# The residual addition of tiles four to eight moves from VectorE to GpSimd

## The chip, the cores and the metric

The kernel runs on one core of one Trainium2 chip. A core has five engines with queues of their own: TensorE (PE in the profile, with its weight loads as PEld), VectorE (DVE), ScalarE (ACT), GpSimd (POOL) and SyncE (SP, which only issues transfers here). They run side by side and wait for each other through semaphores. The metric is the device time of one execution in microseconds (us), the median of several runs.

## The reference, cut to what matters

One inference step of a two-layer backbone, on 256 context tokens and 1024 latent tokens of width 1024, in float32. Each layer ends its mixer with an output projection, a gated residual, a norm and an expert-choice router:

```python
out = jnp.concatenate([y_h, y_a], axis=-1) @ e_w_out[a]      # layer 0; layer 1: o @ r_w_out[r]
x = x + g_a * out                                            # gate product, residual addition
hn = rms_norm(x, norm_ffn_g[l]) * (1.0 + sc_f) + sh_f
x = x + g_f * expert_choice_ffn(hn, router_w[l], moe_w_gu[l], moe_w_down[l])

def expert_choice_ffn(h, router_w, w_gu, w_down):
    cap = CAPACITY_FACTOR * n // N_EXPERTS                   # 2 * n / 16 tokens per expert
    aff = jax.nn.softmax((xf @ router_w).astype(jnp.float32), axis=-1)
    gate, idx = lax.top_k(aff.T, cap)                        # each expert picks its tokens
    xin = xf[idx]
    ...
```

Context and latent tokens are routed apart, so the kernel has three lists to sort: latent tokens in two halves, and context tokens.

## The kernel before, in words

`out_proj_route` is called twice, once per layer, and each call is one stage. It works on ten tiles of 128 tokens: tiles 0 to 3 are the first half of the latent tokens, 4 to 7 the second, 8 and 9 the context. For tile n the engines do this, in turn:

- TensorE projects the tile into a PSUM buffer (line 1415, two buffers in turn).
- VectorE multiplies it with the gate into `xn` (line 1473, semaphore `products`) and adds the residual into `x` (line 1476, semaphore `gated`); the two are `gate_add(n)`. `xn` has two buffers and `x` three.
- ScalarE issues the store of `x` (line 1597), squares and sums it (line 1600), and takes the root (line 1606).
- VectorE inverts the root (line 1480, `invert(n)`).
- ScalarE scales `x` into `xn` again (line 1608, semaphore `scaled`). `xn` then holds the normalised tile.
- GpSimd stores `xn` to HBM (line 1347), and TensorE transposes it (line 1363), for the router's matmuls (line 1376).

After four tiles the router's logits go through a softmax: VectorE lines 1489 to 1497, where `aff_ready` is given, TensorE `to_experts` (line 1392), and VectorE's copy into the work area (line 1504). Then VectorE picks each expert's best tokens, eight at a time: a round is MAX8, FIND_INDEX8 and MATCH_REPLACE8 (lines 1513 to 1515). There are 16 rounds for the first half and 16 for the second, in which the context's list is sorted along.

No scheduler sets the order. Each engine's list is written out by hand, and an engine does its list in order. VectorE's list from tile five on stands in these lines of the kernel before:

```python
            rounds(0, 0, 3)
            gate_add(5)
            rounds(0, 3, 4)
            invert(5)
            rounds(0, 4, 9)
            gate_add(6)
            rounds(0, 9, 10)
            invert(6)
            rounds(0, 10, 15)
            gate_add(7)
            invert(7)
```

Then come the last round of the first half, the second softmax, `gate_add(8)`, the copy `to_work(1)`, `invert(8)`, and the second half's rounds with `gate_add(9)` and `invert(9)` between them. GpSimd has nothing in the stage but the ten stores and, at the end, two gathers by the picked indices (lines 1352 and 1354), with which the expert stage begins.

Of the kernel before, what the change touches and what calls it, by code (L numbers as in the profile page):

```python
# [16 lines left out]
ALU = mybir.AluOpType  # L17
# [1234 lines left out]
PICKS = [(0, CAP[1], CT * P), (CAP[1], CAP[1], (CT + 4) * P), (2 * CAP[1] - CAP[0], CAP[0], 0)]  # L1252
CTX = slice(2 * NE, 3 * NE)
ROUTE_AT = 158016


def out_proj_route(nc, A, S, tag, w, w_in, early_gate, lhs, lhs_in, x_in, x_out, layer, hnT, xn_dram, router, idx, idx_four, gates,
# [4 lines left out]
    NB = 3  # L1262
    NPICK = 2 * CAP[1]
    with ExitStack() as ctx:
        _, ps, sem = scope(nc, ctx, tag)

        def fixed(name, shape, offset, dt=F32):
            return nc.alloc_sbuf_tensor_at(f"{tag}_{name}", shape, dt, offset=offset)
# [3 lines left out]
        x = fixed("x", [P, NB, D], 100672)  # L1272
        xn = fixed("xn", [P, 2, D], 112960)
        junk = fixed("junk", [P, D], 121152)
        work = fixed("work", [3 * NE, LL], ROUTE_AT)
        top = fixed("top", [3 * NE, NPICK], ROUTE_AT + 5120)
        topi = fixed("topi", [3 * NE, NPICK], ROUTE_AT + 6272, U32)
        topf = fixed("topf", [3 * NE, NPICK], ROUTE_AT + 7424)
        back_a = fixed("back_a", [NE, 2, CAP[1]], ROUTE_AT + 8576)
        ge, val, ind = (fixed(n, [NE, CAP[1]], ROUTE_AT + 9600 + 512 * i) for i, n in enumerate(("ge", "val", "ind")))  # L1280
        aff = fixed("aff", [P, 4, NE], ROUTE_AT + 11136)
# [10 lines left out]
        eps_ready, mm, products, gated, squared, v_steps, inverted, rooted, scaled, tr, hn_out = (sem(n) for n in (  # L1292
            "eps_ready mm products gated squared v inverted rooted scaled tr hn_out").split())
        lg_zero, lg_mm, lt_out, tk_tr, subbed, exped, aff_ready, back, worked, a_ready, a_turned, context_turned, picked, finals, idx_ready = (sem(n) for n in (
            "lg_zero lg_mm lt_out tk_tr subbed exped aff_ready back worked a_ready a_turned context_turned picked finals idx_ready").split())
        x_ins, stored = [sem(f"x_in{i}") for i in range(NB)], [sem(f"stored{i}") for i in range(NB)]
# [12 lines left out]
        def tokens(n):  # L1309
            return slice(TILES[n] * P, (TILES[n] + 1) * P)  # L1310
# [4 lines left out]
        @block.sync  # L1315
        def _(sp):
            load_router_w(sp, A, router, layer)
            for n in range(NT):
                if n >= NB:
                    sp.wait_ge(stored[n % NB], 16 * (n // NB))  # L1320
                    sp.wait_ge(scaled, n - NB + 1)
                sp.dma_start(x[:, n % NB, :], x_in(TILES[n])).then_inc(x_ins[n % NB], 16)
                if n == NB:
                    for j in range(4):
                        load_expert(sp, A, layer, expert_w, expert_w_in, j, 0)
            def load_mod(n):
                if n >= 4:
                    sp.wait_ge(mod_used, n - 3)
                src = (A["mod_w"][shift_of, n * P:(n + 1) * P, 0:2048] if n < KD else
                       A["mod_b"][shift_of:shift_of + 1, 0:2048].broadcast_to([P, 2048]))  # L1330
                sp.dma_start(ring[n % 4][:, :, :].rearrange("p j n -> p (j n)"), src).then_inc(mod_in[n % 4], 16)

            if shift_of:
                load_mod(0)
                load_mod(1)
            sp.wait_ge(mm, NT)
            if shift_of:
                for n in range(2, KD + 1):
                    load_mod(n)
            for j in range(4, 9):  # L1340
                load_expert(sp, A, layer, expert_w, expert_w_in, j, 0)

        @block.gpsimd
        def _(pool):
            for n in range(NT):
                pool.wait_ge(scaled, n + 1)
                pool.dma_start(xn_dram[tokens(n), :], xn[:, n % 2, :]).then_inc(xn_stored[n % 2], 16)
            for i in range(2):
                pool.wait_ge(xn_stored[i], 16 * len(range(i, NT, 2)))
            xl, xc, xl_in, xc_in = first  # L1350
            pool.wait_ge(idx_ready, 1)
            pool.indirect_dma_start(xc[:, :], None, xn_dram, bass.IndirectOffsetOnAxis(idx_four[:, 0:1], 0)).then_inc(xc_in, 16)
            pool.wait_ge(idx_ready, 2)
            pool.indirect_dma_start(xl[:, :], None, xn_dram, bass.IndirectOffsetOnAxis(idx[1][:, 0:1], 0)).then_inc(xl_in, 16)
# [110 lines left out]
        def _(dve):  # L1465
            steps = Count(v_steps)

            def gate_add(n):
                dve.wait_ge(mm, n + 1)
                if n >= 2:  # L1470
                    dve.wait_ge(tr, n - 1)
                    dve.wait_ge(xn_stored[n % 2], 16 * (n // 2))
                nc.vector.tensor_tensor(xn[:, n % 2, :], psm[n % 2][:, :], gate[:, 0 if TILES[n] < CT else 1, :], ALU.mult).then_inc(products, 1)
                dve.wait_ge(products, n + 1)
                dve.wait_ge(x_ins[n % NB], 16 * (n // NB + 1))
                nc.vector.tensor_tensor(x[:, n % NB, :], xn[:, n % 2, :], x[:, n % NB, :], ALU.add).then_inc(gated, 1)
# [66 lines left out]
            for n in range(5):  # L1543
                gate_add(n)
                invert(n)
            subtract_max(0)
            shares(0)
            to_work(0)
# [8 lines that stand above are left out]
# [28 lines left out]
            for c in (1, 0):  # L1585
                n = CAP[c]
# [1201 lines left out]
```

## Time and profile before

| | us |
|---|---|
| median of 3 runs (lowest, highest) | 4161.03 (4160.32, 4161.28) |
| the profiled execution's own time | 4160.97 |
| its span in the profile | 4159.2 |
| PE busy | 3887.9 (93%) |
| DVE busy | 1741.3 (42%) |
| ACT busy | 1139.9 (27%) |
| POOL busy | 201.2 (5%) |

The first stage's tiles run from about 905 to 1058 us of the span, the second's from about 3098 to 3240 us. The shares are means over the whole span. In the stages they are others, and what counts there is which wait ends last.

### The profile page before, as it was taken

How to read it: one execution, taken by the hardware profiler on the slowest of the kernel's cores; microseconds unless marked ns; L12 is line 12 of the kernel's file. 1: busy time of each engine (PE TensorE's matmuls, PEld its weight loads, DVE VectorE, ACT ScalarE, POOL GpSimd, SP SyncE). 2: the span in 40 equal slices, each digit the busy share in tenths (PEclk: the TensorE clock that was granted, in tenths of full speed). 3: DMA queues.
4: the chain of work that ended last, by engine and by line, in shares of the span. 5: the costliest groups of instructions: out<-in, count | busy, mean ns of one | idle time of the engine just before them, and what ended most of it. 6: DMA issues, size and time to landing. Idle time of an engine off the chain costs nothing. (4 is left out here: it accounts for less than half of the span.)

```text
span 4159.2 us, 56347 instructions
## 1 busy us (share of the span) xinstructions
PE 3887.9 (93%) x24035; PEld 3135.7 (75%) x24035; DVE 1741.3 (42%) x2860; ACT 1139.9 (27%) x2162; POOL 201.2 (5%) x237
## 2 busy tenths in 40 slices
PE   7999989999799999999899999999879599999998
PEld 3444456654599999997788888888854599999997
DVE  3325457745411111111368788888875411111112
ACT  4010135533201111110444555445534211011112
POOL 1010000000000000000000000000000000000000
PEclk9999989999899999999899999999999899999999
DMA  5432010023888888887210100100223688888886
GB/s 191 142 124 75 16 51 1 1 87 112 278 255 258 260 254 259 253 255 243 80 29 29 30 29 17 35 29 25 83 87 112 207 260 256 262 252 260 252 257 238
DMA packets 507896, 617.88 MB, mean 149 GB/s; under 512 B 17282, under 2 KB 467508, under 8 KB 501632
## 3 DMA queue, kind: packets, MB, share of 16 engines
q1 hardware_dynamic: 482400, 518.89, 38.5%
q0 software_dynamic: 21984, 84.77, 7.3%
q10 hardware_dynamic: 3264, 10.63, 0.6%
q8 instruction: 191, 3.13, 0.3%
q14 instruction: 57, 0.47, 0.0%
HBM read 561.08 MB, written 53.15 MB: 148 GB/s over the span
## 5 line engine op out<-in xcount | busy, mean ns | idle before, releaser
L1855 PEld LDWEIGHTS moe_pgu<-step_hnT,expert_w 128*128 128x128 f32 x8192 | 1113.6, 190 | 20.5 <-issue 20.5
L1855 PE MATMUL moe_pgu<-step_hnT,expert_w 128*128 128x160 f32 x8192 | 1121.7, 299 | 7.3 <-DVE moe_hT L2001 4.2
L2001 DVE TENSOR_TENSOR moe_hT<-moe_sg,moe_pgu 128x160 f32<-128x160 f32 x256 | 82.1, 321 | 968.7 <-PE moe_pgu L1855 959.2
L1867 PE MATMUL moe_pol<-expert_w,moe_hT 128*128 128x256 f32 x2048 | 457.5, 381 | 2.4 <-DVE moe_hT L2001 1.0
L1922 ACT ACTIVATE moe_sg<-moe_pgu 128x160 f32<-128x160 f32 x256 | 77.5, 303 | 1303.4 <-PE moe_pgu L1855 1291.4
L2205 PE MATMUL l_psm<-step_hnT,rec_w 128*128 128x256 f32 x1920 | 425.7, 380 | 3.5 <-ACT l_zc L2288 1.9
L1867 PEld LDWEIGHTS moe_pol<-expert_w,moe_hT 128*128 128x128 f32 x2048 | 383.2, 190 | 59.1 <-DVE moe_hT L2001 10.0
L2205 PEld LDWEIGHTS l_psm<-step_hnT,rec_w 128*128 128x128 f32 x1920 | 362.1, 191 | 51.6 <-ACT l_zc L2288 2.3
L2209 PE MATMUL l_psm<-rec_w,step_hnT 128*128 128x256 f32 x1280 | 282.4, 379 | 0.0
L2209 PEld LDWEIGHTS l_psm<-rec_w,step_hnT 128*128 128x128 f32 x1280 | 240.4, 190 | 31.3
L2013 DVE SCALAR_TENSOR_TENSOR moe_ol<-moe_pol,step_gates,moe_gate_f 128x512 f32<-128x512 f32 x64 | 48.1, 751 | 434.6 <-PE moe_pol L1867 434.6
L2246 PE MATMUL rec_pg<-rec_ring 128*128 128x128 f32 x1600 | 195.4, 280 | 27.8 <-DVE rec_tot L2422 22.2
L2246 PEld LDWEIGHTS rec_pg<-rec_ring 128*128 128x128 f32 x1600 | 189.5, 195 | 40.9 <-issue 32.7
L530 PE MATMUL hin_psm<-step_hnT,hin_w 128*128 128x512 f32 (+1 forms) x576 | 215.9, 531 | 2.7 <-DVE step_hnT L634 2.7
L530 PEld LDWEIGHTS hin_psm<-step_hnT,hin_w 128*128 128x128 f32 x576 | 109.3, 193 | 110.2 <-issue 87.4
L1905 ACT ACTIVATE step_hnT<-moe_pxt,step_modcol 128x128 f32<-128x128 f32 x288 | 108.2, 456 | 177.2 <-PE moe_pxt L1828 177.2
L2543 DVE COPY_PREDICATED rec_AT<-rec_maskb,rec_pg 128x512 f32<-128x512 uint8 (+1 forms) x192 | 109.9, 627 | 46.9 <-PE rec_pg L2246 45.4
L1786 POOL DMA_INDIRECT scratch_xm<-moe_ol,step_idx x31 | 49.1, 1585 | 1443.2 <-DVE moe_ol L2013 1443.2
L1877 PE MATMUL moe_poc<-expert_w,moe_hT 128*32 128x256 f32 x2048 | 117.1, 380 | 0.0
L1118 PE MATMUL att_to_ps<-step_ident,l0a_p 128*128 128x128 f32 x672 | 100.1, 287 | 12.1 <-issue 11.0
L1179 DVE TENSOR_REDUCE att_nmax<-att_s_ps 128x1 f32<-128x1280 f32 (+1 forms) x80 | 99.1, 1274 | 26.6 <-PE att_s_ps L1100 26.1
L1118 PEld LDWEIGHTS att_to_ps<-step_ident,l0a_p 128*128 128x128 f32 x672 | 73.0, 144 | 42.0 <-issue 29.6
(444 smaller groups left out, 4439.5 us busy)
## 6 DMA issues: line engine op xcount, KB each, us to landing
expert_w<-in_moe_w_gu SPq DMA_DIRECT2D x256, 1024.0 KB, 10.4
expert_w<-in_moe_w_down SPq DMA_DIRECT2D x128, 1024.0 KB, 13.4
late_w<-in_mod_w POOLq DMA_DIRECT2D x24, 1024.0 KB, 5.2
rec_w<-in_r_w_in SPq DMA_DIRECT2D x40, 512.0 KB, 3.9
scratch_xm<-op_x ACTq DMA_DIRECT2D x20, 512.0 KB, 2.6
scratch_xn<-op_xn POOLq DMA_DIRECT2D x20, 512.0 KB, 5.5
mod_w<-in_mod_w SPq DMA_DIRECT2D x8, 1024.0 KB, 16.4
op_mod<-in_mod_w SPq DMA_DIRECT2D x8, 1024.0 KB, 7.9
```

What stands on the lines that cost most here:

```text
L530: m = nc.tensor.matmul(psm[j % NPS][:, 0:n * P], w[:, i % 2, k, part, :], hnT[:, k, t0 * P:(t0 + n) * P], start=(k == 0), stop=(k == KD - 1))
L1118: m = nc.tensor.transpose(bank("t", i, g)[:, n * P:(n + 1) * P], p[:, i % 2, r, a * P:(a + 1) * P], S["ident"][:, :])
L1179: nc.vector.tensor_reduce(nmax[:, x:x + 1], s_ps[:, r, 0:nk * P], AX_X, ALU.max, negate=True).then_inc(maxed, 1)
L1855: m = nc.tensor.matmul(pgu[2 * (f % 2) + part][:, :], w[j][:, k, (f % 2) * P:(f % 2 + 1) * P], ring[:, k, e % 8, :], start=(k == 0), stop= ...
L1867: m = nc.tensor.matmul(pol[q // 2][:, (q % 2) * SW:(q % 2 + 1) * SW], hT[:, k, 0:CL], w[8 + q][:, k, :], start=(k == 0), stop=(k == KD - 1))
L1877: m = nc.tensor.matmul(poc[32 * q:32 * q + CP, :], hT[:, k, CL:CC], w[8 + q][:, k, :], start=(k == 0), stop=(k == KD - 1), tile_position=( ...
L1905: r = nc.scalar.activation(dst, src, ACT.Identity, bias=mc[:, layer, 3, c, k:k + 1], scale=mc[:, layer, 4, c, k:k + 1])
L2001: nc.vector.tensor_tensor(hT[:, f, :], sg[:, f % 2, :], pgu[2 * (f % 2) + 1][:, :], ALU.mult).then_inc(multiplied, 1)
L2205: m = nc.tensor.matmul(pz[i % 3][:, 0:2 * P], w[:, k, n // NZU, :], hnT[:, k, c0:c0 + 2 * P], start=(k == 0), stop=(k == KD - 1))
L2209: m = nc.tensor.matmul(pz[i % 3][:, 0:2 * RD], hnT[:, k, t * P:(t + 1) * P], w[:, k, 3:5, :].rearrange("p a c -> p (a c)"), start=(k == 0) ...
L2246: into_banks(h, (d, i), lambda o, t: nc.tensor.matmul(o, kb[:, t * P:(t + 1) * P], qb[:, t * P:(t + 1) * P], start=True, stop=True))
L2543: last = nc.vector.copy_predicated(at, maskb[:, j:j + 1, :].broadcast_to([P, nt, P]), src)
```

## The change

`POOL_ADDS` names tiles 4 to 8. For those, GpSimd does the residual addition in front of its store of the same tile, waiting for the gate product and for the loaded residual. VectorE's `gate_add` returns after the gate product. Everything else in VectorE's list keeps its place. Before the addition of tile 9, VectorE waits for `gated` of tile 8, which keeps the count of that semaphore in order.

```diff
+POOL_ADDS = range(4, 9)
...
             for n in range(NT):
+                if n in POOL_ADDS:
+                    pool.wait_ge(products, n + 1)
+                    pool.wait_ge(x_ins[n % NB], 16 * (n // NB + 1))
+                    nc.gpsimd.tensor_tensor(x[:, n % NB, :], xn[:, n % 2, :], x[:, n % NB, :], ALU.add).then_inc(gated, 1)
                 pool.wait_ge(scaled, n + 1)
                 pool.dma_start(xn_dram[tokens(n), :], xn[:, n % 2, :]).then_inc(xn_stored[n % 2], 16)
...
                 nc.vector.tensor_tensor(xn[:, n % 2, :], psm[n % 2][:, :], gate[:, 0 if TILES[n] < CT else 1, :], ALU.mult).then_inc(products, 1)
+                if n in POOL_ADDS:
+                    return
+                if n - 1 in POOL_ADDS:
+                    dve.wait_ge(gated, n)
                 dve.wait_ge(products, n + 1)
                 dve.wait_ge(x_ins[n % NB], 16 * (n // NB + 1))
                 nc.vector.tensor_tensor(x[:, n % NB, :], xn[:, n % 2, :], x[:, n % NB, :], ALU.add).then_inc(gated, 1)
```

VectorE's list in the first stage, before, from the third round to the fifth, around tile five (`op_xn<-op_psm,op_gate` is the gate product, `op_x<-op_xn,op_x` the addition, `op_rstd` the inverted root):

```order
L1515 MATCH_REPLACE op_work<-op_top,op_work 16x512
L1473 TENSOR_TENSOR op_xn<-op_psm,op_gate 128x1024
L1476 TENSOR_TENSOR op_x<-op_xn,op_x 128x1024
L1513 MAX op_top<-op_work 16x8
L1514 MAX_INDEX op_topi<-op_top,op_work 16x8
L1515 MATCH_REPLACE op_work<-op_top,op_work 16x512
L1480 RECIPROCAL op_rstd<-op_ssq 128x1
```

The same place now (the lines count nine or five more):

```order
L1524 MATCH_REPLACE op_work<-op_top,op_work 16x512
L1478 TENSOR_TENSOR op_xn<-op_psm,op_gate 128x1024
L1522 MAX op_top<-op_work 16x8
L1523 MAX_INDEX op_topi<-op_top,op_work 16x8
L1524 MATCH_REPLACE op_work<-op_top,op_work 16x512
L1489 RECIPROCAL op_rstd<-op_ssq 128x1
```

The addition is gone from between the product and the fourth round, and the reciprocal still stands behind that round. It is the same at tile six, and at tiles seven and eight no round stands between.

GpSimd's list in the first stage now, from its start to the second addition (`scratch_xn<-op_xn` is the store; before, the ten stores stood in one piece):

```order
L1352 DMA scratch_xn<-op_xn 128x1024 x4
L1350 ISA
L1350 TENSOR_TENSOR op_x<-op_xn,op_x 128x1024
L1352 DMA scratch_xn<-op_xn 128x1024
L1350 TENSOR_TENSOR op_x<-op_xn,op_x 128x1024
L1352 DMA scratch_xn<-op_xn 128x1024
```

Each addition stands right in front of the store of its own tile. The row ISA in front of the first addition is new, and the second stage has none.

## Rows read from the trace of the kernel before

**Rows 1.** Waits of DVE, 980 to 1045 us: total, times, longest
```profile
DVE op_stat L1489 <- PE op_tok L1382: 8.9, 1, 8.9
DVE op_rstd L1480 <- ACT op_ssq L1606: 5.8, 3, 2.7
```

**Rows 2.** Timeline of DVE, first stage: start, us, what [idle before <-releaser]
```profile
963.67 1.23 DVE L1473 TENSOR_TENSOR op_xn<-op_psm,op_gate 128x1024 f32<-128x1024 f32 x1 [10.04 <-PE op_psm L1415]
...
971.49 0.23 DVE L1497 TENSOR_TENSOR op_aff<-op_aff,op_stat 128x64 f32<-128x64 f32 x1
...
983.76 1.22 DVE L1473 TENSOR_TENSOR op_xn<-op_psm,op_gate 128x1024 f32<-128x1024 f32 x1
985.02 1.22 DVE L1476 TENSOR_TENSOR op_x<-op_xn,op_x 128x1024 f32<-128x1024 f32 x1
...
989.51 0.16 DVE L1480 RECIPROCAL op_rstd<-op_ssq 128x1 f32<-128x1 f32 x1 [1.23 <-ACT op_ssq L1606]
...
1004.88 0.16 DVE L1480 RECIPROCAL op_rstd<-op_ssq 128x1 f32<-128x1 f32 x1
...
1020.11 0.16 DVE L1480 RECIPROCAL op_rstd<-op_ssq 128x1 f32<-128x1 f32 x1 [1.91 <-ACT op_ssq L1606]
...
1035.78 0.67 DVE L1504 COPY op_work<-op_pback 16x512 f32<-16x512 f32 x1
1039.13 0.16 DVE L1480 RECIPROCAL op_rstd<-op_ssq 128x1 f32<-128x1 f32 x1 [2.68 <-ACT op_ssq L1606]
```

**Rows 3.** Timeline of ACT, first stage
```profile
986.28 0.33 ACTq L1597 DMA_DIRECT2D scratch_xm<-op_x  x1
...
989.71 1.15 ACT L1608 ACTIVATE op_xn<-op_x,op_rstd 128x1024 f32<-128x1024 f32 x1 [0.30 <-DVE op_rstd L1480]
...
1004.40 0.30 ACT L1606 ACTIVATE op_ssq<-op_ssq,op_eps 128x1 f32<-128x1 f32 x1
...
1019.78 0.29 ACT L1606 ACTIVATE op_ssq<-op_ssq,op_eps 128x1 f32<-128x1 f32 x1
```

**Rows 4.** Timeline of PE, first stage and the expert stage's first transposes
```profile
975.95 0.60 PE L1392 MATMUL op_pback<-step_ident,op_aff 128*16 128x128 f32 x4
...
1007.21 3.60 PE L1415 MATMUL op_psm<-op_w,l_filt 128*128 128x512 f32 x8
...
1021.50 1.27 PE L1363 MATMUL op_pst<-step_ident,op_xn 128*128 128x128 f32 x8 [3.83 <-ACT op_xn L1608]
1022.57 5.16 PE L1415 MATMUL op_psm<-op_w,l_filt 128*128 128x512 f32 x8
...
1094.10 1.09 PE L1837 MATMUL moe_pxt<-step_ident,first_xc 128*128 128x128 f32 x4 [10.73 <-PEq L80]
```

**Rows 5.** Timeline of POOL, first stage
```profile
955.11 0.53 POOL L1347 DMA_DIRECT2D scratch_xn<-op_xn  x1 [14.08 <-ACT op_xn L1608]
...
991.15 0.53 POOL L1347 DMA_DIRECT2D scratch_xn<-op_xn  x1 [20.90 <-ACT op_xn L1608]
...
1084.44 1.03 POOL L1352 DMA_INDIRECT first_xc<-scratch_xn,step_idx_four  x1 [25.09 <-DVE step_idx L1587]
```

**Rows 6.** Windows: us, PE, PEld, DVE, ACT, POOL busy (x), PEclk, DMA, GB/s
```profile
1021.50:1026.00 4.50, 4.50 (x13) 2.57 (x14) 1.22 (x5) 2.90 (x8) 0.53 (x1) 0.62 0.29 117
1026.00:1031.00 5.00, 5.00 (x73) 2.83 (x72) 0.00 (x0) 1.32 (x2) 0.00 (x0) 1.00 0.01 3
```

**Rows 7.** Timeline of DVE, second stage: reciprocals of tiles five, six and eight
```profile
3171.63 0.16 DVE L1480 RECIPROCAL op_rstd<-op_ssq 128x1 f32<-128x1 f32 x1 [1.23 <-ACT op_ssq L1606]
...
3187.00 0.16 DVE L1480 RECIPROCAL op_rstd<-op_ssq 128x1 f32<-128x1 f32 x1
...
3221.10 0.16 DVE L1480 RECIPROCAL op_rstd<-op_ssq 128x1 f32<-128x1 f32 x1 [2.67 <-ACT op_ssq L1606]
```

**Rows 8.** Tile op_x, and groups of DVE by form: durations in ns
```profile
L1476 DVE TENSOR_TENSOR op_x<-op_xn,op_x x20: 1224/1225/1226, 906.6 to 3235.3; 128x1024 f32<-128x1024 f32 x20
...
L2458 DVE TENSOR_TENSOR_SCAN rec_X<-rec_restart,l_zc 128x1280 f32<-128x1280 uint8 x16 | 45.2, 2825 | 0.6
```

## The prediction

> **What bounds the kernel now.** I read the timelines of the five engines over the first stage first, then the waits of VectorE, then the same places in the second stage, and last the prices of single instructions. I name tiles from zero, as the code does.
>
> The reader is to see one chain of waits through the tiles five to eight, and to ask at each reciprocal whether VectorE came late or early. The chain is: gate product, residual addition, store issue, square and root on ScalarE, reciprocal on VectorE. VectorE's list is in order, so the rounds behind a reciprocal start only when it is done. At tile five the addition starts at 985.02, ScalarE issues the store at 986.28, and VectorE, done with its fourth round, idles 1.23 us before the reciprocal at 989.51 until the root is there [rows 2, 3]. At tile seven it idles 1.91 us and at tile eight 2.68 us for the same reason [rows 2]. These three make the 5.8 us that VectorE waits for roots in this stretch [rows 1]. At tile six it idles nothing: the root ends at 1004.70 and the reciprocal starts at 1004.88, while at tile seven it starts 0.04 us behind its root (1020.07 to 1020.11) [rows 2, 3]. So the root had only some 0.14 us to spare at tile six. VectorE is busy there, and yet the additions are not what holds it: the chain to the root is.
>
> What is late next is read from PE. It idles 3.83 us until `xn` of tile seven is scaled, and only then transposes it [rows 4]. Behind that stand the router's matmuls of the second half, and VectorE idles 8.9 us for them [rows 1]. So a delay at tiles five, six and seven goes on through PE to the second softmax and to tile eight's product. A delay at tile eight goes on through the reciprocal to the second half's rounds, to the indices, to GpSimd's first gather (1084.44) [rows 5], and to the expert stage, whose first transposes start at 1094.10 [rows 4]. From there on PE is the busy engine, so I count every microsecond at the stage's end as one at the program's end. The second stage shows the same idle times: 1.23 us at tile five, none at six, 2.67 us at eight [rows 7].
>
> **The change part by part.** Removed from VectorE: five additions a stage, each 1.225 us [rows 8]. I cost this at nothing gained. The rounds that move up end earlier and then wait for the root, as the rows say they do already at tile five; at tile six the freed time becomes a wait as well, beyond the 0.14 us; at tiles seven and eight nothing but the copy into the work area stands between product and reciprocal.
>
> Added to the chain: the way over GpSimd. Before, from the end of the product (983.76 plus 1.22, so 984.98) to ScalarE's store issue (986.28) it is 1.30 us [rows 2, 3]. Now it is the wake-up of GpSimd, the addition there, and the wake-up of ScalarE. The first I take from GpSimd's stores: `xn` is scaled at 990.86 (989.71 plus 1.15), and its store starts on GpSimd at 991.15, 0.29 us later [rows 3, 5]. The last I take as VectorE's, 0.04 us (the addition's end at 986.24 to 986.28).
>
> The addition's own time on GpSimd is the unknown, as no elementwise instruction of this size on that engine is in the trace. From below, VectorE's row: 1.225 us. From above, the slowest row by element: the scan takes 2.825 us for 1280 elements a partition, 2.21 ns each, so 2.26 us for 1024, and twice that, 4.52 us, if each of the two operands costs a pass at this pace [rows 8]. I take 2.45 us, two passes at VectorE's pace, one for each operand, which lies next to the scan's 2.26 us.
>
> With it the way is 0.29 + 2.45 + 0.04 = 2.78 us instead of 1.30, so 1.48 us more per tile. With the lower end it is 0.25 us more, with the upper 3.55.
>
> Beside this value stands a rule. The Trainium skill (GPSIMD Engine Reference, "Performance versus the Vector engine") gives a float32 addition of 2048 elements as 1.96 times slower on GpSimd than on VectorE, and says that plain elementwise work belongs on VectorE. By it an estimate for this addition is 2.40 us, and the time would be 0.4 us below my sum. No run here shows it yet.
>
> Now tile by tile, in each stage:
>
> Tile four: hidden. Its reciprocal and the first softmax come 1.48 us later, but the shares are ready at 971.72 and PE asks for them at 975.95 [rows 2, 4]. That is 4.23 us of cover. If it were gone, the tile would cost its 1.48 us like the others.
>
> Tile five: 1.48. Tile six: 1.48 less the 0.14 to spare, so 1.34. Tile seven: 1.48. Tile eight: 1.48, the copy into the work area being done while VectorE waits. Together 5.78 us a stage, 11.56 for both.
>
> New waits: on GpSimd each addition waits for its product, and only the store of the same tile is queued behind it, which comes after the addition in any case. The stores of the tiles before have been issued long ago (at 955.11 for tile three, while tile four's product ends at 964.9) [rows 2, 5]. VectorE's new wait at tile nine is met, since the reciprocal of tile eight already needed that addition. The loads of `x` wait for scaled tiles three back, come some microseconds later, and are still in time: VectorE takes up tile nine's product after the next six rounds.
>
> PE's longer idle: the granted clock is 0.62 of full speed on the mean over 1021.5 to 1026, after the 3.83 us without work, and 1.00 after that, that is, it falls to the lower of the two levels and comes back [rows 6]. Eight matmuls take 5.16 us there, against 3.60 us at the full clock [rows 4], so it costs 1.56 us already. The idle time grows by about 1.5 us. I cost this at nothing, since the clock is already down; were the low stretch as long again, it would be 1.56 us a stage, up to 3.1 in all.
>
> The profiled execution took 4160.97 us, against 4161.03 for the median. The sum is 4160.97 + 11.56 = 4172.5 us. With the addition at 1.225 us it would be 4162.7 (2 x (4 x 0.25 - 0.14) = 1.7), at 4.52 us 4189.1 (2 x (4 x 3.55 - 0.14) = 28.1).
>
> **The rivals.** I count as no change what lies within 0.2%, 8.3 us, which is about what a measurement of this kernel can tell.
>
> First, GpSimd adds about as fast as VectorE. The place is the same chain, and its price per tile is the addition's time less 0.97 us. Below about 2.05 us for one addition the eight prices come to less than 8.3 us, and it decides for no change; at 1.225 the time is 4162.7. For it speaks that nothing in the trace shows GpSimd slow on such work; against it, that its single records, stores of 0.53 us and gathers of 1.03 us [rows 5], do not show it fast either.
>
> Second, the first addition of all is late. The order shows a new row ISA in front of it, without a tile, on GpSimd. It stands behind tile three's store, so it has from 955.64 to 964.9, 9.3 us, before the first addition is asked for, and the 4.23 us of tile four behind that. For this to cost anything, it must hold the addition by more than 2.75 us beyond its product (4.23 less 1.48). If it took as long as that cover, 9.3 us, and began only with the product, the first stage would lose 6.5 us more (9.3 less 2.75): 4179.0.
> The Trainium skill (GPSIMD Engine Reference, "Instruction dispatch") says that the first call of a freshly loaded GpSimd program costs about 6 us that no record shows. By that rule, a load that begins only at the call would cost 3.25 us beyond the cover (an estimate of 4175.8), and one that begins at the row ISA nothing. No run here shows it yet.
>
> Third, GpSimd is far slower than two passes, or is held up by the rounds that now run beside it at tiles five and six. At the upper end it is 4189.1.
>
> Fourth, the freed time counts after all. Were VectorE's own work the limit at tiles five to eight, eight additions of 1.225 us would be won, 9.8 us: 4151.2. The idle times in front of three reciprocals of four speak against it.
>
> **How the numbers follow.** My forecast, an addition from 2.05 to 3 us on the chain, gets 0.70, and its own range is 4169.3 to 4176.9. The first rival gets 0.15, the second 0.07, the third 0.06, the fourth 0.02. The forecast, the second and the third are slower by over 0.2%: 0.83. The first is the same: 0.15. Faster: 0.02. The range for 8 in 10 starts at 4167, which takes in an addition of 1.75 us, and so the upper part of the first rival. It ends at 4180, which takes in the second, and an addition of 3 us with the clock's 3.1 us more.
>
> **What would show it.** Right: five additions a stage on GpSimd of 2.2 to 2.7 us each; 2.5 to 3.1 us from the end of the product to the store issue; VectorE idle in front of the reciprocals of tiles five, six, seven and eight by about 3.9, 2.5, 4.6 and 4.3 us; PE idle over 5 us before tile seven's transposes; the first expert transposes 5 to 7 us later against the first tile of their stage, in both stages. Wrong: a tile five reciprocal as early as before; PE waiting for the first softmax at 975.95 (the cover of tile four gone); a stage that gives back at its end what the tiles lost; or additions under 2 us.

## The result, and the profile after

The changed kernel takes 4177.68 us (median of 6 runs, 4173.96 to 4178.91), where the kernel before took 4161.64 us beside it (6 runs, 4160.32 to 4168.36). The ratio is 1.0032, with a 95% interval of 1.0021 to 1.0043. That is 13.3 us slower, with 8.7 to 17.9 us as its interval; the two medians lie 16.0 us apart, which is inside it. The forecast was 4172.5 us, with a range from 4167 to 4180.

The profiled execution took 4178.44 us, with a span of 4176.7. PE is busy for 3901.9 us (3887.9 before), DVE for 1728.5 (1741.3), POOL for 225.1 (201.2). So GpSimd took over what VectorE gave up, and it needed about twice as long for it.

The timeline of POOL shows the new work, in the columns of [rows 5]:

```profile
969.83 2.34 POOL L1350 TENSOR_TENSOR op_x<-op_xn,op_x 128x1024 f32<-128x1024 f32 x1 [9.35 <-DVE op_xn L1478]
...
989.93 2.34 POOL L1350 TENSOR_TENSOR op_x<-op_xn,op_x 128x1024 f32<-128x1024 f32 x1 [13.62 <-DVE op_xn L1478]
...
1007.68 2.35 POOL L1350 TENSOR_TENSOR op_x<-op_xn,op_x 128x1024 f32<-128x1024 f32 x1 [9.93 <-DVE op_xn L1478]
...
1024.15 2.33 POOL L1350 TENSOR_TENSOR op_x<-op_xn,op_x 128x1024 f32<-128x1024 f32 x1 [9.93 <-DVE op_xn L1478]
```

An addition takes 2.34 us, whether the rounds run beside it (tiles five and six, at 989.93 and 1007.68) or not (tile seven, at 1024.15). On VectorE it took 1.225 [rows 8].

How it stands on the chain is seen around tile five, first on VectorE and then on ScalarE, which answers to the store issue of [rows 3]:

```profile
988.61 1.23 DVE L1478 TENSOR_TENSOR op_xn<-op_psm,op_gate 128x1024 f32<-128x1024 f32 x1
...
995.53 0.17 DVE L1489 RECIPROCAL op_rstd<-op_ssq 128x1 f32<-128x1 f32 x1 [3.67 <-ACT op_ssq L1615]
...
1012.00 0.16 DVE L1489 RECIPROCAL op_rstd<-op_ssq 128x1 f32<-128x1 f32 x1 [2.39 <-ACT op_ssq L1615]
...
1028.39 0.16 DVE L1489 RECIPROCAL op_rstd<-op_ssq 128x1 f32<-128x1 f32 x1 [4.33 <-ACT op_ssq L1615]
...
1049.29 0.16 DVE L1489 RECIPROCAL op_rstd<-op_ssq 128x1 f32<-128x1 f32 x1 [4.08 <-ACT op_ssq L1615]
```

```profile
992.30 0.33 ACTq L1606 DMA_DIRECT2D scratch_xm<-op_x  x1
```

The product ends at 989.84 (988.61 plus 1.23), GpSimd starts 0.09 us later, ends at 992.27, and the store is issued at 992.30. The way is 2.46 us; before it was 1.30. VectorE idles 3.67, 2.39, 4.33 and 4.08 us before the four reciprocals, where it idled 1.23, 0, 1.91 and 2.68 [rows 2]. At tiles five, six and seven that is 2.39 to 2.44 us more: the 1.23 us of the addition that it was relieved of, and the 1.16 us by which the way has grown.

PE, against [rows 4]:

```profile
1029.79 1.97 PE L1368 MATMUL op_pst<-step_ident,op_xn 128*128 128x128 f32 x8 [4.99 <-ACT op_xn L1617]
1031.55 5.18 PE L1420 MATMUL op_psm<-op_w,l_filt 128*128 128x512 f32 x8
...
1104.39 1.09 PE L1846 MATMUL moe_pxt<-step_ident,first_xc 128*128 128x128 f32 x4 [11.33 <-PEq L80]
```

PE idles 4.99 us before tile seven's transposes (3.83 before), and these take 1.97 us instead of 1.27. From 1029.80 to 1031.60 the granted clock is 0.50, the lower of its two levels.

Subtracting these times from those of before would mislead. Tile four's product starts at 968.52 here and at 963.67 in [rows 2], 4.85 us later, and nothing on GpSimd has changed up to there. The windows of this execution, in the columns of [rows 6], show where that comes from, with two stretches of the first layer:

```profile
320.00:340.00 20.00, 18.26 (x43) 8.24 (x43) 8.57 (x13) 3.44 (x5) 0.00 (x0) 0.80 0.18 62
490.00:500.00 10.00, 10.00 (x27) 6.00 (x27) 1.40 (x4) 0.87 (x2) 0.00 (x0) 0.73 0.04 13
```

The same stretches of the kernel before:

```profile
320.00:340.00 20.00, 18.26 (x50) 8.95 (x50) 10.12 (x14) 3.62 (x5) 0.00 (x0) 0.94 0.20 62
490.00:500.00 10.00, 10.00 (x37) 6.22 (x36) 0.00 (x0) 0.60 (x2) 0.00 (x0) 1.00 0.05 15
```

The granted clock is 0.80 and 0.73 where it was 0.94 and 1.00, and fewer matmuls are done in the same time. The first question of the experiments was whether the change brings that.

### The profile page after: what moved, and what is told of

It is laid out like the page before. It is cut to its first block and busy times, and to the rows that moved or that the text cites. A ratio compares the mean times of both kernels' runs of the same rounds, so it can differ in the third digit from the quotient of the medians.

```text
span 4176.7 us, 56349 instructions
## 1 busy us (share of the span) xinstructions
PE 3901.9 (93%) x24035; PEld 3145.4 (75%) x24035; DVE 1728.5 (41%) x2850; ACT 1140.8 (27%) x2162; POOL 225.1 (5%) x247
## 5 line engine op out<-in xcount | busy, mean ns | idle before, releaser
L1914 ACT ACTIVATE step_hnT<-moe_pxt,step_modcol 128x128 f32<-128x128 f32 x288 | 108.4, 457 | 177.0 <-PE moe_pxt L1837 177.0
## 6 DMA issues: line engine op xcount, KB each, us to landing
expert_w<-in_moe_w_gu SPq DMA_DIRECT2D x256, 1024.0 KB, 10.4
```

The source lines that it names most:

```text
L1914: r = nc.scalar.activation(dst, src, ACT.Identity, bias=mc[:, layer, 3, c, k:k + 1], scale=mc[:, layer, 4, c, k:k + 1])
```

## The experiments

Theory A is the prediction's: the additions on the chain of tiles five to eight are the whole cost. Its rival, theory B: a GpSimd instruction of this kind in the program also slows what runs ahead of it. In each experiment the kernel before ran on the same chip beside the others. In the table a stage's length is read from the timeline of the profiled execution, from the first gate product of the stage to GpSimd's first gather, so that it holds nothing of what lies outside it.

| kernel | median us (runs) | ratio, 95% interval | stage 1, us | stage 2, us |
|---|---|---|---|---|
| before | see below | | 179.13 | 168.85 |
| changed, the runs above | 4177.68 (6) | 1.0032 [1.0021, 1.0043] | 183.98 | 174.14 |
| e1, before again | 4165.26 (11) | 1.0002 [0.9993, 1.0011] | 179.13 | 169.46 |
| e2, changed again | 4176.6 (6) | 1.0032 [1.0020, 1.0044] | 183.50 | 174.15 |
| e3, first stage only | 4173.97 (7) | 1.0025 [1.0014, 1.0036] | 183.79 | 169.15 |
| e4, one small addition | 4164.69 (11) | 0.9997 [0.9988, 1.0006] | 177.00 | 168.88 |
| e5, before, list filled | 4147.41 (5) | 0.9959 [0.9946, 0.9972] | 171.80 | 161.65 |
| e6, changed, list filled | 4156.0 (9) | 0.9976 [0.9966, 0.9986] | 173.22 | 163.20 |
| e7, added twice | 4196.38 (5) | 1.0071 [1.0058, 1.0084] | 193.15 | 182.19 |
| e8, shared | 4168.51 (12) | 1.0007 [0.9998, 1.0015] | 180.56 | 171.98 |
| e9, tiles zero to four | 4170.44 (11) | 1.0016 [1.0007, 1.0025] | 177.01 | 170.66 |
| e10, in turn | 4178.06 (6) | 1.0030 [1.0016, 1.0044] | 183.40 | 172.99 |
| e11, beside the product | 4167.04 (11) | 0.9999 [0.9990, 1.0008] | 179.60 | 168.59 |
| e12, tiles two to four | 4167.17 (11) | 1.0000 [0.9991, 1.0009] | 176.99 | 168.75 |

The kernel before had medians of 4165.0 us (24 runs) beside e1 to e4, 4165.59 (21) beside e5 to e8, 4165.59 (22) beside e9 to e11, and 4167.1 (15) beside e12.

### The two kernels once more (e1, e2)

No edit: the kernel before and the changed kernel as they are.

> The kernel before, unchanged. Theory A (the additions on the chain are the whole cost; what the profiled execution lost ahead of the first stage, 4.9 us, and between the stages, 1.7 us, are single stretches in which TensorE ran at its lower clock, and they differ from execution to execution whatever the kernel): ratio 1.000, and the first gate product of the first stage, at 905.3 us in the profile of before, comes somewhere between 903 and 911. Theory B (a GpSimd instruction of this kind in the program slows what runs ahead of it too): ratio 1.000, and that product comes at 905.3 within 1 us, as in before.

> The changed kernel, unchanged. Theory A: the two stages lose 10.3 us together (five chains of 1.15 us a stage, of which tile four's is hidden, and some 0.5 us of TensorE's lower clock); the time is 8 to 17 us above before as the clock stretches fall, and the first gate product lies in the same range as that of the kernel before run again. Theory B: 16 us above before, the first gate product at 910 within 1 us.

Measured: no difference for the one, with its first gate product at 905.26 us, and 13.3 us more (8.3 to 18.3) for the other. In this second execution of the changed kernel, VectorE's timeline starts tile four at the same time as [rows 2]:

```profile
963.67 1.22 DVE L1478 TENSOR_TENSOR op_xn<-op_psm,op_gate 128x1024 f32<-128x1024 f32 x1 [10.05 <-PE op_psm L1420]
...
990.67 0.16 DVE L1489 RECIPROCAL op_rstd<-op_ssq 128x1 f32<-128x1 f32 x1 [3.66 <-ACT op_ssq L1615]
...
1007.14 0.16 DVE L1489 RECIPROCAL op_rstd<-op_ssq 128x1 f32<-128x1 f32 x1 [2.39 <-ACT op_ssq L1615]
...
1023.53 0.16 DVE L1489 RECIPROCAL op_rstd<-op_ssq 128x1 f32<-128x1 f32 x1 [4.33 <-ACT op_ssq L1615]
...
1044.12 0.16 DVE L1489 RECIPROCAL op_rstd<-op_ssq 128x1 f32<-128x1 f32 x1 [4.09 <-ACT op_ssq L1615]
```

So these rows may be subtracted: 989.51 to 990.67, 1004.88 to 1007.14, 1020.11 to 1023.53, 1039.13 to 1044.12 [rows 2]. That is 1.16, 2.26, 3.42 and 4.99 us: one step of 1.10 to 1.16 for each of tiles five, six and seven, and 1.57 for tile eight, with the slower matmuls after tile seven in it. At the first gather 4.37 us are left (1088.81, against 1084.44 in [rows 5]); of the 0.62 us given back, 0.50 are tile nine's transposes, which took 1.59 us before and take 1.09 here. The window from 320 to 340 us is back at a clock of 0.93. So one and the same changed kernel reaches its first product at 910.16 us in one execution and at 905.31 in another: the 4.85 us ahead of the stage belong to that execution and not to every execution of the change.

### One stage alone, and the instruction alone (e3, e4)

```diff
-                if n in POOL_ADDS:
+                if layer == 0 and n in POOL_ADDS:
```

> GpSimd adds in the first stage alone; the second is as before. Theory A: half of the cost, 5.2 us above before, with the clock stretches on top or not. Theory B: the part ahead of the first stage is lost as well, 5 + 5 = 10 us above before.

The stages did as expected: the first is 4.7 us longer, the second is as before. The time is 10.4 us longer by the ratio (5.8 to 15.0), so over 5 us more than the stages show, and the interval just leaves the expected 5.2 out; by the medians it is 9.0 us. The mean granted clock of these runs is 0.9703, against 0.9722 for before beside them. e4, e9, e10 and e12 come back to this excess.

```diff
+                if n == 4 and layer == 0:
+                    pool.wait_ge(products, n + 1)
+                    nc.gpsimd.tensor_tensor(spare[:, 0:1], eps[:, 0:1], eps[:, 0:1], ALU.add)
```

> All residual additions on VectorE as before; GpSimd does one addition of a single column (128x1) into a spare place, once, in the first stage, behind the store of tile three and the product of tile four. It brings the row ISA into the program. Theory A: no change, within 2 us of before. Theory B: 5 us above before, and the first gate product at 910.

All residual additions are VectorE's here. There is no difference, and the first product of the first stage is nevertheless at 910.88 us (905.31 before). The place of that product is thus as theory B had it, and the time is not: its 5 us over before lie outside the interval of -5.0 to 2.5 us. One small elementwise instruction on GpSimd costs nothing that can be measured.

The profiled executions alone would not clear theory B. The three kernels without such an instruction on GpSimd reach the product at 905.3 (before), 905.3 (e1) and 905.9 us (e5); of the eleven with one, only e2 does (905.3), and the others come at 907.9 to 916.5. Each is a single execution. What speaks against a price for the instruction's presence is the times of all executions: e4, e11 and e12 are not slower than before, with upper ends of 2.5, 3.3 and 3.8 us, and e2's profile shows that the changed kernel can be as early as before.

### The waits filled (e5, e6)

```diff
-            rounds(0, 3, 4)
+            rounds(0, 3, 5)
             invert(5)
-            rounds(0, 4, 9)
+            rounds(0, 5, 8)
             gate_add(6)
-            rounds(0, 9, 10)
+            rounds(0, 8, 10)
             invert(6)
-            rounds(0, 10, 15)
+            rounds(0, 10, 13)
             gate_add(7)
+            rounds(0, 13, 14)
             invert(7)
-            rounds(0, 15, 16)
+            rounds(0, 14, 16)
...
             to_work(1)
+            rounds(1, 0, 1)
             invert(8)
-            rounds(1, 0, 6)
+            rounds(1, 1, 6)
```

> All additions on VectorE, its list of rounds moved: one round more stands between a product and its reciprocal at tiles five to eight, in both stages. The idle times in front of the reciprocals (1.23, 0, 1.91, 2.67 us before) are then filled, the product of tile seven comes two rounds earlier, and PE's 3.83 us without work at tile seven go, and with them the 1.56 us of low clock. Theory A (the chain from product to reciprocal is what the stages wait for at these tiles): 3.83 + 1.56 + some 2.1 of the 2.67 at tile eight, about 7.5 us a stage, so 15 us less: 4150. The rival (VectorE's own work is the limit, the idle times are only where it shows): no gain, 4165.

This is the version that beats both: 4147.41 us, 17.1 us under before by the ratio (11.7 to 22.5). The stages are 7.3 and 7.2 us shorter, 14.5 together, against 15 expected. The waits of VectorE from 980 to 1055 us, against [rows 1]:

```profile
DVE op_stat L1489 <- PE op_tok L1382: 5.6, 1, 5.6
...
DVE op_rstd L1480 <- ACT op_ssq L1608: 0.5, 1, 0.5
```

The waits for roots have shrunk from 5.8 us to 0.5. The windows around tile seven show what that was worth, against [rows 6]:

```profile
1010.00:1016.00 6.00, 6.00 (x15) 2.66 (x14) 5.01 (x10) 2.49 (x7) 0.00 (x0) 1.00 1.01 420
1016.00:1021.00 5.00, 5.00 (x19) 2.61 (x18) 4.79 (x14) 2.83 (x7) 0.53 (x1) 1.00 0.39 160
```

PE has no idle time left there, and its clock stays at 1.00, the higher of its two levels. PE is now the bound at these tiles.

e6 is the same edit in the changed kernel.

> The changed kernel with the same moved rounds as e5. Theory A: the rounds now cover most of the longer way over GpSimd; idle is left only where the way is longer than one round of cover (after, it idles 3.67, 2.39, 4.33, 4.08 us in front of the four reciprocals, a round is some 2.7 us): some 1, 0, 1.6 and 1.9 us, so 1 to 3.5 us a stage over e5, 2 to 7 in both. The rival (GpSimd's additions cost by being there, through VectorE's instructions beside them or the code they bring): it stays as far over e5 as the changed kernel is over before, 12 to 15 us.

The stages are 1.42 and 1.55 us longer than in e5, 2.97 together, where the changed kernel's were 4.37 and 5.30 longer than before's. With the same additions on GpSimd, two thirds of their cost has gone. Waits of VectorE from 990 to 1065 us:

```profile
DVE op_rstd L1489 <- ACT op_ssq L1617: 6.1, 4, 2.4
```

What is left are waits for roots again, 6.1 us against the 0.5 of e5; only 1.42 us of them are left at the stage's end. By the ratios e6 is 7.1 us over e5, and the two intervals together leave 0.3 to 13.9 us for that, so the 3 us of the stages are inside. With the list filled, too, the additions are better left on VectorE.

### Added twice (e7)

```diff
+                    nc.gpsimd.tensor_tensor(x[:, n % NB, :], x[:, n % NB, :], spare[:, 0:1].broadcast_to([P, D]), ALU.add).then_inc(twice, 1)
+                    pool.wait_ge(twice, n - POOL_ADDS[0] + 1)
                     nc.gpsimd.tensor_tensor(x[:, n % NB, :], xn[:, n % 2, :], x[:, n % NB, :], ALU.add).then_inc(gated, 1)
```

> The changed kernel with a second GpSimd instruction of the same size (a zero column added to x) ahead of each of the ten additions, on the chain. Theory A: 2.34 us and a short wait, say 2.4, more at tiles five to eight of both stages, and tile four still hidden (1.15 + 2.4 = 3.55 of its 4.23 us of cover): 8 x 2.4 = 19 us over the changed kernel, so 4196, and VectorE idles 2.4 us longer in front of each of the four reciprocals. Rival one (only the hand-over to GpSimd and back is what costs, the addition's length is covered): about 4177. Rival two (the rounds on VectorE slow the second instruction or are slowed by it): over 4200.

The timeline of POOL at tile five, and of VectorE behind it:

```profile
989.50 1.88 POOL L1354 TENSOR_TENSOR op_x<-op_x,op_spare 128x1024 f32<-128x1024 f32 x1 [11.60 <-DVE op_xn L1484]
991.46 2.34 POOL L1356 TENSOR_TENSOR op_x<-op_xn,op_x 128x1024 f32<-128x1024 f32 x1
```

```profile
997.06 0.17 DVE L1495 RECIPROCAL op_rstd<-op_ssq 128x1 f32<-128x1 f32 x1 [5.63 <-ACT op_ssq L1622]
```

The instruction with the repeated column takes 1.88 us and not 2.34, so a tile gets 1.96 us more (989.50 to 991.46). VectorE idles 5.63 us where it idled 3.67, the same 1.96. Against e2 the stages are 9.65 and 8.04 us longer, 17.7 together; by the ratios the two kernels are 16.3 us apart. Four times 1.96 is 7.84, which the second stage shows: there each microsecond on GpSimd at tiles five to eight is one at the end. The 1.8 us that the first stage has over that stand on PE, in slower matmuls of the same kind: the eight behind tile seven's transposes take 5.63 us where e2 has 4.87 (granted clock 0.63 from 1037.0 to 1042.5, against 0.73 in e2), and tile nine's transposes 1.93 us where e2 has 1.09. Tile four carried the 1.96 us as well, and tile five's product is still 78.45 us behind the first, as before: there it is hidden, as predicted.

### Shared, in turn, and beside the product (e8, e10, e11)

In e8 VectorE and GpSimd each add a part of the columns of tiles five to eight.

```diff
-POOL_ADDS = range(4, 9)
+POOL_ADDS = range(5, 9)
+ON_DVE = 640
...
+                    nc.gpsimd.tensor_tensor(x[:, n % NB, ON_DVE:], xn[:, n % 2, ON_DVE:], x[:, n % NB, ON_DVE:], ALU.add).then_inc(other, 1)
...
+                m = ON_DVE if n in POOL_ADDS else D
+                nc.vector.tensor_tensor(x[:, n % NB, 0:m], xn[:, n % 2, 0:m], x[:, n % NB, 0:m], ALU.add).then_inc(gated, 1)
```

> At tiles five to eight VectorE adds columns 0 to 639 and GpSimd at the same time 640 to 1023; the other tiles are VectorE's alone. Theory A: GpSimd's 384 columns take 384/1024 of 2.34, so 0.88 us, with the wake-up 0.96, and VectorE's 640 take 0.77: the way from product to store issue is 1.0 us where it was 1.30 before, 0.3 us less at four tiles in two stages, 2.4 us less: 4163. Rival one (the two engines' reads of the same memory stand in each other's way, so that one addition waits for the other): 0.77 + 0.96 = 1.73 us, 0.45 us more a tile, 3.6 us more: 4169. Rival two (any GpSimd instruction on the chain costs about the same): as the changed kernel, 4177.

POOL at tile five of e8, and VectorE:

```profile
989.97 1.62 POOL L1352 TENSOR_TENSOR op_x<-op_xn,op_x 128x384 f32<-128x384 f32 x1 [14.83 <-DVE op_xn L1480]
```

```profile
988.66 1.23 DVE L1480 TENSOR_TENSOR op_xn<-op_psm,op_gate 128x1024 f32<-128x1024 f32 x1
989.92 0.82 DVE L1484 TENSOR_TENSOR op_x<-op_xn,op_x 128x640 f32<-128x640 f32 x1
```

My theory of 0.88 us for 384 columns fell: GpSimd took 1.62, and ended at 991.59, 0.85 us after VectorE's 640 columns (990.74). The time, 2.9 us over before by the ratio (-0.8 to 6.2), holds what the first rival gave (3.6 more), and no change as well; it leaves out theory A's 2.4 us less and the second rival's 12 more. What tells is the row, and a fixed part in every GpSimd addition would look the same there. So e10 makes VectorE wait for GpSimd:

```diff
+                if n in POOL_ADDS:
+                    dve.wait_ge(other, n - POOL_ADDS[0] + 1)
                 nc.vector.tensor_tensor(x[:, n % NB, 0:m], xn[:, n % 2, 0:m], x[:, n % NB, 0:m], ALU.add).then_inc(gated, 1)
```

> As e8, but VectorE waits for GpSimd's 384 columns before it adds its 640, so the two never add at the same time. Theory L (in e8 GpSimd's 1.62 us are 0.74 us of waiting for VectorE's addition and 0.88 us of adding): GpSimd's row is 0.9 us, the way from product to store issue 0.08 + 0.9 + 0.04 + 0.82 + 0.04 = 1.9 us instead of 1.66 in e8 and 1.30 before, 0.2 us a tile over e8, so 4169.5 to 4171. The rival F (a GpSimd addition has a fixed part of some 1.2 us and 384 columns cost 1.62 us alone, too): the way is 2.6 us, 1.3 us a tile over before, 10 us over before: 4175.

POOL at tile five of e10, and VectorE:

```profile
989.86 0.99 POOL L1352 TENSOR_TENSOR op_x<-op_xn,op_x 128x384 f32<-128x384 f32 x1 [14.83 <-DVE op_xn L1480]
```

```profile
988.54 1.23 DVE L1480 TENSOR_TENSOR op_xn<-op_psm,op_gate 128x1024 f32<-128x1024 f32 x1
990.98 0.82 DVE L1486 TENSOR_TENSOR op_x<-op_xn,op_x 128x640 f32<-128x640 f32 x1 [1.21 <-POOL op_x L1352]
```

Alone, 384 columns take 0.99 us. Theory L holds in the row, and F is out: 0.63 of e8's 1.62 us were waiting for VectorE's addition. The time of 4178.06 is over both of L's ends. The way came out at 2.06 us (from 989.77 to the store issue at 991.83) instead of the 1.9 I expected, that is 0.76 more than before's 1.30. In e8 it was 1.80 us (989.89 to 991.69), and not the 1.66 I had named. The stages of e10 are 4.27 and 4.14 us longer, 8.4 together, and the interval of 6.7 to 18.3 us holds that, while the middle of it, 12.5, is again some 4 us over.

e11 lets GpSimd add beside VectorE's product instead, which reads one operand from PSUM:

```diff
+                if n in POOL_ADDS:
+                    nc.vector.tensor_tensor(xn[:, n % 2, m:], psm[n % 2][:, m:], gate[:, g, m:], ALU.mult).then_inc(high, 1)
+                nc.vector.tensor_tensor(xn[:, n % 2, 0:m], psm[n % 2][:, 0:m], gate[:, g, 0:m], ALU.mult).then_inc(products, 1)
```

> At tiles five to eight VectorE makes the product of columns 640 to 1023 first (some 0.56 us) and then that of 0 to 639 (0.82); GpSimd adds the first part while VectorE makes the second, which reads one operand from PSUM. Theory L (only an addition with both operands in SBUF holds GpSimd up): GpSimd's row is 0.9 us and ends as VectorE's addition begins; from the product's start to the store issue 0.56 + 0.82 + 0.82 + 0.1 = 2.3 to 2.4 us, where it was 2.53 before and 2.9 in e8: VectorE idles 1.0 to 1.1 us at tile five (1.23 before), and the time is 1 to 2 us under before: 4163. Rival F (fixed part): GpSimd's row is 1.6 us though nothing stands beside it. Rival P (VectorE's product holds it up as the addition did): GpSimd's row is 1.6 to 1.7 us, it ends with VectorE's addition or behind it, and the time is before's or 2 us over it.

POOL at tile five of e11, and VectorE:

```profile
995.57 0.99 POOL L1352 TENSOR_TENSOR op_x<-op_xn,op_x 128x384 f32<-128x384 f32 x1 [14.17 <-DVE op_xn L1483]
```

```profile
994.93 0.56 DVE L1483 TENSOR_TENSOR op_xn<-op_psm,op_gate 128x384 f32<-128x384 f32 x1
995.40 0.81 DVE L1484 TENSOR_TENSOR op_xn<-op_psm,op_gate 128x640 f32<-128x640 f32 x1
996.25 0.99 DVE L1487 TENSOR_TENSOR op_x<-op_xn,op_x 128x640 f32<-128x640 f32 x1
```

GpSimd's addition ran at its own 0.99 us beside the product, as L said. VectorE's addition came 0.31 us before GpSimd was done (995.57 plus 0.99 is 996.56), and now it is the one that is longer, 0.99 instead of 0.82 us. The Trainium skill (SBUF — State Buffer, "Who interferes with whom") says that a VectorE instruction with two SBUF inputs contends with a GpSimd instruction that reads SBUF, that the shared ports are an exclusive lock for which the order of issue decides who blocks, and that a VectorE instruction with at most one SBUF input, outside its two-port modes, does not contend. e8, e10 and e11 agree for who waits and who does not. The wait they show is some 0.14 us shorter than what was left of the other's instruction: 0.63 of 0.77 us in e8, 0.17 of 0.31 in e11. The way from the product's start to the addition's end is 2.31 us, against 2.48 before. VectorE's idle time at tile five is 1.23 us as before, and not the 1.0 to 1.1 I expected: what stands behind the addition moves up with it. The expected microsecond or two can't be told from no change: the ratio is 0.9999, and the stages are 0.5 us longer and 0.3 us shorter.

### Where nothing waits (e9, e12)

```diff
-POOL_ADDS = range(4, 9)
+POOL_ADDS = range(0, 5)
```

> GpSimd adds for tiles zero to four, VectorE for five to nine: as many additions on GpSimd as in the changed kernel, ten of 2.34 us, but at tiles where VectorE idles some 10 us for the next projection. Theory A (an addition costs only where the next step waits for its tile): no change, 4165, at most 1 us more. The rival (something that comes with full-size additions on GpSimd costs wherever they stand, as the few microseconds that the changed kernel is over the sum of its two stages might say): 4168 to 4177.

The ten additions of 2.34 us at these tiles cost 6.7 us by the ratio (2.9 to 10.4), and by theory A they should have cost 1 at most. Part of it I had overlooked. In the second stage VectorE does not idle for a projection after tile zero; the root is what it waits for before the next product. First before, then e9, on VectorE:

```profile
3098.07 1.23 DVE L1473 TENSOR_TENSOR op_xn<-l_psm,op_gate 128x1024 f32<-128x1024 f32 x1 [2.78 <-PE l_psm L1415]
...
3103.78 0.16 DVE L1480 RECIPROCAL op_rstd<-op_ssq 128x1 f32<-128x1 f32 x1 [3.22 <-ACT op_ssq L1606]
3103.86 1.20 DVE L1473 TENSOR_TENSOR op_xn<-l_psm,op_gate 128x1024 f32<-128x1024 f32 x1
```

```profile
3103.43 1.23 DVE L1478 TENSOR_TENSOR op_xn<-l_psm,op_gate 128x1024 f32<-128x1024 f32 x1 [2.99 <-PE l_psm L1420]
...
3110.38 1.21 DVE L1478 TENSOR_TENSOR op_xn<-l_psm,op_gate 128x1024 f32<-128x1024 f32 x1
```

The second product follows after 6.95 us instead of 5.79: 1.16 us, one way over GpSimd. The rest of the 6.7 does not stand in the stages (177.01 and 170.66 us). Therefore e12 kept only the tiles that are hidden in both stages:

```diff
-POOL_ADDS = range(4, 9)
+POOL_ADDS = range(2, 5)
```

> GpSimd adds for tiles two, three and four only, six additions in all. In e9 the products of these tiles and all behind them stood as before in the first stage, and in the second the shift of 1.16 us came with tiles zero and one. Theory A: no stage is longer, 4165, and e9's 4.85 us are 1.2 of tile zero and the rest the spread between executions. The rival (full-size additions on GpSimd lower the granted TensorE clock elsewhere in the program, 0.971 on the mean of e9's runs where before had 0.972): 3 to 4 us over before again, 4168 to 4170, with the stages as long as before.

No difference: 1.0000, 0.9991 to 1.0009, and stages of 176.99 and 168.75 us. Six full-size additions on GpSimd that nobody waits for cost nothing that can be measured. The rival's 3 to 4 us lie at the upper end of the interval (3.8 us), and the mean granted clock is 0.9717, against 0.9721 for before beside it: nothing here speaks for the rival, and its lower end is not quite shut out.

## Why the prediction was right, point by point

**The chain through tiles five to eight: right.** The result lies in the range and on the side that had 0.83, and e6, e7 and e12 each turn the same handle. More on GpSimd costs its full length (e7), less waiting behind the chain gives most of it back (e6), and additions off the chain cost nothing (e12). VectorE's idle times came out as forecast: 3.9, 2.5, 4.6 and 4.3 were named, 3.67, 2.39, 4.33 and 4.08 were read. The first expert transposes come 5.44 and 5.21 us later against the first product of their stage, where 5 to 7 were named. Two signs fell just short: the way is 2.46 us (2.5 to 3.1 named), and PE idles 4.99 us before tile seven (over 5 named).

**The price per tile: too high.** I put the way over GpSimd at 2.78 us, and it was 2.46. The wake-up was taken from a store (0.29 us), and for an addition it is 0.09; the addition was taken as two passes (2.45 us), and is 2.34. So a tile costs 1.16 and not 1.48, and two stages 9.1 us (2 x (3 x 1.15 + 1.10)), not 11.56. The Trainium skill's ratio of 1.96 (GPSIMD Engine Reference, "Performance versus the Vector engine") gave an estimate of 2.40 us; the measured ratio is 1.91.

**The clock: not shown either way, and the total lands partly by luck.** I cost PE's longer idle time at nothing, since the clock falls there already. In the first stage of both executions of the changed kernel tile seven's transposes ran at the lower level, 1.97 us instead of 1.27. But in the second stage they took 1.97 us in the kernel before, 1.09 in e1, 1.78 in the changed kernel and 1.60 in e2, so the runs do not show that the longer idle time is what costs. The two stages of e2 are 9.67 us longer than before's, about 0.6 us more than the chain's 9.1. The measured 13.3 us lies nearer to the forecast's 11.56 than to this sum, and that is luck: the interval reaches down to 8.3, and the too high price, some 2.5 us in all, stood in for time that the chain does not explain.

**Tile four hidden: right**, with one addition (the change) and with two (e7).

**The rivals.** GpSimd as fast as VectorE fell with the row of 2.34 us. The late first addition fell too: it starts at 969.83, 0.08 us after its product, as the others do. Of the row ISA the trace shows, under the addition's line:

```profile
L1350 POOLq MODIFY_POOL_CONFIG  x2: 42/42/42, 960.5 to 960.5; - x2
```

It stands right behind tile three's store (959.95 plus 0.53), and GpSimd's 9.35 us of idle time follow it, so what it sets off is hidden there, or small. The Trainium skill (GPSIMD Engine Reference, "Instruction dispatch") has some 6 us for a first call: a load that begins at this row would fit into the 9.35 us, and one that begins only at the call is excluded by the addition's start. A GpSimd held up by the rounds fell, with 2.34 and 2.35 us beside them and 2.33 without; what does hold it up is VectorE's addition (e8), which this change never puts beside it. That the freed time counts fell in this kernel: at tiles five to seven the waits took it all.

**What stays open.** e3, e9 and e10 are some 4 to 5 us over what their stages show (for e9 over the second stage's 1.8), and the mean granted clock of their runs is 0.9703, 0.9708 and 0.9702 against 0.9722 and 0.9723 for before beside them. In e4, e11 and e12, which also use GpSimd, the excess is missing (0.9733, 0.9732, 0.9717), so the mere presence of its work does not bring it. The record shows what the excess goes with. Among the 82 executions of the kernel before beside the experiments, the 13 with a mean granted clock of 0.970 took 4170.4 us on the mean and the 11 with 0.975 took 4161.6, which is about 1.7 us for each 0.001. An estimate that takes the others to the same clock by this figure puts e3 at 6 us over before, e10 at 8 and e9 at 3, where their stages show 5.0, 8.4 and 1.8; and the changed kernel at 7 to 8 us, where its chain is 9.1. By this estimate most of what the times show over the stages goes with a lower clock. What gave these runs the lower clock I have not found, nor whether the change has a part in it, and it is part of the 13.3 us.

## What to carry to other kernels

Before moving work to an idle engine, ask whether the engine that it leaves is what the next step waits for: read the idle time in front of the instructions behind it. If they wait already, as here, the freed time becomes more waiting, and the slower engine's price goes onto the chain. Here the same idle times named the better edit: put independent rounds between the product and the reciprocal that waits (e5). And VectorE and GpSimd, both adding from SBUF, did not add side by side (e8, e10); beside a VectorE instruction that reads one operand from PSUM GpSimd's addition ran at its own length (e11).

## What the runs showed of the hardware that was not expected

An addition on GpSimd takes 2.34 us for 1024 columns and 0.99 for 384, and 1.88 us for 1024 if one operand is a repeated column. An estimate from the first two is 2.1 ns for a column and 0.2 us for the instruction.

The clock does not always fall after the same idle time. In [rows 4] PE idles 3.83 us before tile seven and the granted clock falls to 0.62 [rows 6]. In e12 it idles as long, as PE's timeline and the windows show:

```profile
1032.49 1.09 PE L1368 MATMUL op_pst<-step_ident,op_xn 128*128 128x128 f32 x8 [3.83 <-ACT op_xn L1617]
1033.42 3.60 PE L1420 MATMUL op_psm<-op_w,l_filt 128*128 128x512 f32 x8
```

```profile
1032.00:1036.50 4.50, 4.00 (x16) 2.27 (x16) 1.71 (x5) 3.32 (x9) 0.53 (x1) 1.00 0.28 117
```

The clock stays at 1.00, and the eight matmuls take 3.60 us and not 5.16. A first stage of 179.13 us becomes one of 177.0 in e4, e9 and e12: 1.7 us of that come here, and the other 0.4 at tile nine's transposes, which take 1.59 us in before and 1.10 in e12. The kernel before shows the same by itself: in its second stage PE also idles 3.83 us before tile seven, and the transposes then take 1.97 us in one execution and 1.09 in the other (e1). And ahead of the first stage the same instructions reached its first product at times from 905.3 to 916.5 us in the profiled executions of all the kernels: single profiles of this kernel differ by several microseconds before the place that is looked at, so a stage is measured from its own start.
